# Input and up projections with the activations stationary: 512 weight columns stream, and TensorE turns the result back

## The reference

```
h = rms_norm(x, norm1_w);  proj = h @ w_in            # 2048 -> 5648: q, k, v, z, xbc (conv), dt
   attention (8 heads), SSD scan (16 heads)
x = x + concat(attn, ssm) @ w_out                     # 2048 -> 2048
h = rms_norm(x, norm2_w)
u = causal_dwconv(h @ w_up, ffn_conv_w, ffn_conv_b)   # 2048 -> 2 x 5632, 3 taps over positions
x = x + (silu(u_gate) * u_val) @ w_down               # 5632 -> 2048
second layer: mod = silu(c) @ w_ada + b_ada           # 2048 -> 6144, one row
h = rms_norm(x) * (1 + scale) + shift;  proj = h @ w_in_2   # 2048 -> 7168
   dilated attention (8 heads), retention (4 heads), gates
x = rms_norm(x + gate * (y @ w_out_2))
```

## Time and profile before

| | |
|---|---|
| median of 2 runs | 1643.15 us (1641.5 to 1644.81) |
| the profiled execution | 1646.69 us |
| its span, first to last instruction | 1645.0 us |
| TensorE matmul, VectorE, ScalarE busy | 1597.3, 1159.6, 807.7 us |
| mean granted clock of TensorE | 0.992 |
| HBM read | 332.8 MB, 204 GB/s over the span |

### The profile page before, as it was taken

One profiled execution on the slowest core, in us unless ns is written; L12 is line 12 of the kernel. 1 busy time (PEld: TensorE's weight loads), 2 busy tenths in 40 slices (PEclk: granted clock), 3 DMA queues, 4 the chain that ended last, 5 costly groups with the idle time before them and its releaser, 6 DMA issues.

```text
span 1645.0 us, 33704 instructions
## 1 busy us (share of the span) xinstructions
PE 1597.3 (97%) x13254; PEld 1567.6 (95%) x13254; DVE 1159.6 (70%) x1357; ACT 807.7 (49%) x973; POOL 26.3 (2%) x53
## 2 busy tenths in 40 slices
PE   7999999999999999999999999999799999999997
PEld 7998899989999999999999999999799999999996
DVE  6676677765678988888888888667664544664755
ACT  6444355544554545545545455444454544454542
POOL 0000000000000000000000000000000000000000
PEclk9999999999999999999999999999899999999999
DMA  9353344455548777787777875555455555455451
GB/s 347 137 180 129 128 153 142 154 184 185 184 160 335 271 271 297 258 303 274 258 290 270 302 288 188 189 187 183 141 188 185 189 184 168 139 170 174 156 180 52
DMA packets 85187, 336.17 MB, mean 204 GB/s; under 512 B 9456, under 2 KB 9712, under 8 KB 78704
## 3 DMA queue, kind: packets, MB, share of 16 engines
q1 hardware_dynamic: 77328, 281.05, 49.5%
q0 software_dynamic: 7056, 51.38, 8.5%
q10 hardware_dynamic: 720, 2.52, 0.4%
HBM read 332.82 MB, written 2.10 MB: 204 GB/s over the span
## 4 chain that ended last, share of the span: by engine, by line
PE 72%; DVE 5%; issue 2%; ACT 1%; DVEq 0%; ACTq 0%
PE PS L1097 23%; PE PS L1101 23%; PE PS L1099 23%; DVE ada_w L932 1%; DVE wlo L587 1%; ACT whi L255 1%; PE PS L1198 1%; DVE UV L890 1%; PE PS L1165 1%; PE PS L1343 0%; DVE X L1084 0%; PE PS L1184 0%; DVE rb L621 0%; DVE X L603 0%; PE PS L1144 0%
## 5 line engine op out<-in xcount | busy, mean ns | idle before, releaser
L1097 PE MATMUL PS<-gh,whi 128*128 128x256 f32 x3520 | 998.9, 284 | 14.6 <-DVE wlo L587 9.6
L1099 PE MATMUL PS<-gl,whi 128*128 128x256 f32 x3520 | 984.5, 280 | 0.0
L1101 PE MATMUL PS<-gh,wlo 128*128 128x256 f32 x3520 | 984.3, 280 | 0.0
L587 DVE TENSOR_TENSOR wlo<-raw,whi 128x1024 fp32r<-128x1024 f32 x528 | 644.7, 1224 | 421.1 <-ACT whi L255 420.0
L255 ACT ACTIVATE whi<-raw 128x1024 fp32r<-128x1024 f32 x528 | 557.7, 1060 | 718.5 <-PE PS L1101 716.1
L1097 PEld LDWEIGHTS PS<-gh,whi 128*128 128x128 f32 x3520 | 665.8, 189 | 21.9 <-issue 20.6
L1099 PEld LDWEIGHTS PS<-gl,whi 128*128 128x128 f32 x3520 | 667.2, 190 | 2.8 <-issue 1.9
L1101 PEld LDWEIGHTS PS<-gh,wlo 128*128 128x128 f32 x3520 | 667.4, 190 | 0.0
L1097 PE MATMUL PS<-ah,whi 128*128 128x256 f32 x704 | 198.8, 282 | 10.8 <-DVE UV L890 7.2
L1099 PE MATMUL PS<-al,whi 128*128 128x256 f32 x704 | 197.3, 280 | 0.0
L1101 PE MATMUL PS<-ah,wlo 128*128 128x256 f32 x704 | 197.3, 280 | 0.0
(11 more groups left out here) (187 smaller groups left out, 793.9 us busy)
## 6 DMA issues: line engine op xcount, KB each, us to landing
raw<-weights SPq DMA_DIRECT2D x528, 512.0 KB, 3.4
ada_w<-w_ada POOLq DMA_DIRECT2D x48, 1024.0 KB, 5.2
outT<-X SPq DMA_DIRECT2D x4, 512.0 KB, 2.6
X<-xT SPq DMA_DIRECT2D x3, 512.0 KB, 8.7
c<-const ACTq DMA_DIRECT2D x1, 1536.0 KB, 6.3
c_act<-c_rows POOLq DMA_DIRECT2D x1, 1024.0 KB, 9.0
X<-xT SPq DMA_DIRECT2D x2, 256.0 KB, 5.0
prm<-params ACTq DMA_DIRECT2D x1, 276.5 KB, 4.3
```

The source lines that it names most:

```text
L587: dve.tensor_tensor(wlo[:, j % SPLIT, :], raw[:, j, :], whi[:, j % SPLIT, :].bitcast(F32), ALU.subtract).then_inc(s_lo, 1)
L1097: pe.matmul(out[:, t, :], whi[:, b, w], hi[:, kt, :], start=first and half == 0 and t % 2 == 0, stop=False, skip_group_check=True)
L1099: pe.matmul(out[:, t, :], whi[:, b, w], lo[:, kt, :], start=False, stop=False, skip_group_check=True)
L1101: mm = pe.matmul(out[:, t, :], wlo[:, b, w], hi[:, kt, :], start=False, stop=last and half == 1, skip_group_check=True)
```

## The change

The input projections of both layers and the up projection use `product_natural`: now a tile of the activations (128 channels by 128 positions) is stationary and 512 weight columns stream, for each of 2 row tiles and 2 halves of the positions three matmuls, 12 per unit. A group then lies natural in its two banks: positions on the partitions, 512 channels along the free axis. It is turned back in these steps:

- ScalarE copies the two banks to SBUF (`natural`, in the up projection `ffn_natural` in two halves with the inverse root as its scale per partition), before the split of that slot.
- TensorE does the first unit of the next group and then eight transposes of 128x128 (`turn`). In the projections they write back into the group's own two banks, in the up projection into banks 4 and 5 (gate) and 6 and 7 (value). The value's turn stands behind the first unit of the down projection.
- `land` (VectorE, layer 1) and `landed2` (ScalarE, layer 2) take the turned group out, one slot later than before. In the up projection nothing is copied again: base and taps read PSUM, and the taps leave out the columns ahead of the first position, so that UG and UV with their zero columns go.

The inverse root of the second norm is needed per partition: `sum_columns` multiplies each half of the squares (stationary) with one column of ones, after the sixth unit of the first gate group. The convolution steps of layer 1 (`ssm_base`, `ssm_silu`, `ssm_taps`) come one slot later. The ada tiles are spread anew: 8 ahead of the loop (3 in the slots of the output projection, 5 in the first feed-forward step), then 4 in each of the 10 loop steps.

```diff
-        UG, o = place("UG", [P, 4, S + 2], offset=area)
-        UV, o = place("UV", [P, 4, S + 2], offset=o)
-        CG, o = place("CG", [P, 4, S], offset=o)
+        UN, o = place("UN", [P, 2, 4, S], offset=area)
+        CG, o = place("CG", [P, 4, S], offset=o + 64)
...
+            def natural(k, last, par, dst):
+                act.wait_ge(s_used, last + 1 + SPLIT)
+                act.activation(dst, acc_tiles(par), ACT.Copy).then_inc(s_nat, 1)
...
+            def ffn_natural(val, last, grp, par):
+                act.wait_ge(s_used, last + 1 + SPLIT)
+                act.wait_ge(s_evac, grp + 2)
+                for c in range(2):
+                    ins = act.activation(UN[:, val, 2 * c:2 * c + 2, :], acc_tiles(par)[:, 2 * c:2 * c + 2, :], ACT.Copy,
+                                         scale=r2[:, c:c + 1])
+                    ins.then_inc(s_unat, 1)
+                act.sem_inc(s_evac, 1)
...
             for n in range(IN_SLOTS):
+                if n % 8 == 7:
+                    natural(n // 8, 8 * B_IN + n, (G_IN + n // 8) % 2, landing1(n // 8))
                 split(B_IN, LEAD + n)
...
+            def landed2(g):
+                act.wait_ge(s_turn, 11 + g + 1)
+                act.activation(QB[:, 4 * g:4 * g + 4, :], acc_tiles((G_IN2 + g) % 2), ACT.Copy).then_inc(s_evac, 1)
...
             def land(g):
-                finished(8 * (B_IN + g) + 7, G_IN + g)
+                dve.wait_ge(s_turn, g + 1)
...
-                    if ada and j in (0, 3, 6):
-                        ada_tile(i, j // 3)
-                ffn_evac(unit + 7, grp, G_FF % 2, UG)
+                    if j in (3, 7):
+                        ada_tile(i, j // 4)
...
-                    if ada and j in (0, 6, 7):
-                        ada_tile(i, 3 + (0, 6, 7).index(j))
-                ffn_evac(unit + 15, grp + 1, (G_FF + 1) % 2, UV)
+                    if j in (0, 6):
+                        ada_tile(i, 2 + j // 6)
...
+            def product_natural(b, par, tiles, first, last):
+                for half in range(2):
+                    kt = tiles[half]
+                    w = slice(512 * half, 512 * half + 512)
+                    for c in range(2):
+                        rows = slice(P * c, P * c + P)
+                        out = PS[:, 2 * par + c, :]
+                        pe.matmul(out, gh[:, kt, rows], whi[:, b, w], start=first and half == 0, stop=False)
+                        pe.matmul(out, gh[:, kt, rows], wlo[:, b, w], start=False, stop=False)
+                        mm = pe.matmul(out, gl[:, kt, rows], whi[:, b, w], start=False, stop=last and half == 1)
+                mm.then_inc(s_used, 1)
+
+            def turn(src, dst, signal):
+                for c in range(2):
+                    for t in range(4):
+                        mm = pe.transpose(dst[:, t, P * c:P * c + P],
+                                          src[:, 2 * c + t // 2, P * (t % 2):P * (t % 2) + P], ident)
+                mm.then_inc(signal, 1)
...
+            def whole(blk, grp, par, need, after_first=None):
                 pe.wait_ge(s_evac, grp + 1)
+                for u in range(8):
+                    pe.wait_ge(s_lo, blk * 8 + (u + 1))
+                    pe.wait_ge(s_gl, need(2 * u + 1))
+                    product_natural(u % SPLIT, par, (2 * u, 2 * u + 1), u == 0, u == 7)
+                    if u == 0 and after_first is not None:
+                        ffn_turn(after_first, 0)
...
+            def sum_columns(buf):
...
+                    for c in range(2):
+                        mm = pe.matmul(PS[:, 4 + c, 0:1], buf[:, t // 4, t % 4, P * c:P * c + P], ones[:, 0:1],
+                                       start=(t == 0), stop=(t == 7))
...
             for n in range(IN_SLOTS):
                 stream_in(B_IN, G_IN, n, lambda kt: kt + 1)
+                if n % 8 == 0 and n:
+                    turned_back(n // 8 - 1, (G_IN + n // 8 - 1) % 2, landing1(n // 8 - 1))
                 slot1(n)
```

More of the change, by code:

```diff
@@ L965, in ffn @@
                         ffn_product(i)
-            dve.wait_ge(s_c, 1)
-            with dve.Fori(1, 1 + ADA_TILES // ADA_STEP) as i:
-                ffn(i, True)
-            for i in range(1 + ADA_TILES // ADA_STEP, FF_GROUPS):
+            with dve.Fori(1, last) as i:
                 ffn(i)
+            ffn(last)
             dve.wait_ge(s_ada, ADA_TILES)
@@ L1103, in product @@
                 mm.then_inc(s_used, 1)
-            def group(unit, j0, units, grp, par, hi, lo, need):
-                pe.wait_ge(s_evac, grp + 1)
-                for u in range(units):
-                    pe.wait_ge(s_lo, unit + (u + 1))
-                    if need is not None:
-                        pe.wait_ge(s_gl, need(2 * u + 1))
-                    product((j0 + u) % SPLIT, acc_tiles(par), (2 * u, 2 * u + 1), u == 0, u == units - 1, hi, lo)
-            def whole(blk, grp, par, need):
-                group(blk * 8, 0, 8, grp, par, gh, gl, need)
+            def product_natural(b, par, tiles, first, last):
[9 more added lines that the diff above has]
+                mm.then_inc(s_used, 1)
```

203 lines of the change are left out of this document (130 added, 73 removed).

## The result

The changed kernel takes 1673.7 us (median of 2 runs, 1673.12 to 1674.27) against 1643.15: a ratio of 1.022, 95% interval 1.018 to 1.027. It is 30.5 us slower where 40.5 us less were forecast. The miss is 71 us. Two runs each are few, for the kernel before ranges from 1631 to 1648 us over all its later runs. But both runs of the changed kernel are above 1673 us: it is slower, and only whether by more or less than 2% is unclear.

What follows compares the result with a forecast made beforehand. The prediction took TensorE's 128-column weight load to bound each pair, hiding the stream. Terms of -73.6 + 41.4 - 8.5 + 0.2 = -40.5 us gave a forecast of 1603 us from 1643.15, range 1592 to 1630 us.

Steps and rivals of the forecast that it cites:

- Natural products: Input and up projections: 4512 matmuls of 512 columns at 215.5 ns replace 9024 of 256, saving 73.6 us.
- The nearest rows: Earlier trace's F32 sum-of-squares instructions, 215 ns each, and 256-column matmuls at 1.2 GHz, 213 ns, taken to price wide products.
- rival 2: Wide products cost by the streamed column, 226.7 to 235.6 ns each: 1653 to 1693 us; loses from 224.5 ns; chance 0.08.
- Rival 1: Each change of weights costs wide products extra, 219.9 or 224.4 ns each: 1623 or 1643 us; chance 0.13.
- Turning back: Eight transposes for each of 47 groups on TensorE, 110 ns each: 41.4 us added.
- The copy: ScalarE's accumulator copy before each turn, 1.01 us, covered by the next group's first unit of 2.59 us: no cost.
- rivals 3 and 4: Late copies at 15 of 25 projection turns, +15 to +45 us (0.07); transposes at 274 ns latency, +62 us (0.02).
- Feed-forward on VectorE: Down projection's eight waits for UV and their restarts go, saving 8.5 us; 3.6 us at the last hi/lo split stays.
- One value wherever they stand: Sign to look for: 512-column F32R matmuls start 215 to 216 ns apart, the same in every stretch.
- What remains: The 152 units still using `product` keep about 421 us, -8 to +8 us, counted at nothing.
- Taps, base, alignment: Taps and base cost the same from PSUM as from SBUF, and activations keep their address offset: nothing added.

Runs made afterwards that it cites:

- e8: Changed kernel with 128 (first input projection) or 192 (up projection) streamed columns under 128-column loads, and 2 x 256 under 64-column loads (second input projection): 1521.1 us.
- e1: Changed kernel with streamed weights 320 columns wide in the first input projection, 384 in the up projection, 2 x 256 in the second input projection: 1528.0 us.
- e12: Changed kernel, middle units: up projection operands read as two-byte bfloat16, second input projection streaming one F32R column 512 times: 1653.5 us.
- e2: Changed kernel with weights stationary and 512 activation columns streaming in the second input projection, and alternating banks in the up projection: 1681.2 us.
- e3: Changed kernel with smaller stationary loads, 64 columns in the second input projection and 32 in the up projection: 1678.0 us.
- e7: Kernel before with only the new spread of the ada tiles: 1644.5 us, ratio 1.003 to the kernel before.
- e11: Kernel before run once more, unchanged: 1643.7 us.
- e13: Kernel before with the new ada spread and a redundant 512-column F32 matmul at three places: 1616.5 us, ratio 0.987 to the kernel before.
- e16: Kernel before with the new ada spread and a redundant 512-column F32R matmul ahead of each feed-forward step: 1619.7 us.
- e17: Changed kernel with a redundant 512-column F32 matmul at the second group of every down projection in the loop: 1675.1 us, ratio 1.022 to the kernel before.

## Why the prediction was wrong

- *Natural products, the step that failed.* The step had 215.5 ns; 230.3 were measured: +66.8 us. The change of stationary and moving was to save 73.6 us and saved 7. The step rested on the reading of the earlier trace rows, that a load of 113 ns bounds today's pair and hides its stream. e8 refutes it. A load of 128 columns and a stream of 256 are nearly equally long, so a row at 113 ns could not tell them apart, and I took the one that was written beside it.
- *The nearest rows.* The earlier trace rows read at half the rate, and I had said so myself, for rival 2. They have the same cycles but not the same bytes per time. The bound that speaks at full rate stood in the earlier trace rows: 0.443 ns a column.
- *Rival 2* gave 226.7 to 235.6 ns and 1653 to 1693 us, and is what happened (228.9 and 233.3 ns, 1674 us), at a chance of 0.08 where it deserved the most. Its mechanism was half right: the cost goes with the columns (e1, e8) and, as far as e12 tells, comes from reading new columns of SBUF, not from the streamed buffers being written (e2). Its other points held: the change loses from 224.5 ns on.
- *Rival 1*, a cost of each change of weights: out by the 216.3 ns of e12, with the same loads, and by e3, where a load of 32 columns leaves 231.6 ns. Against it speaks also the 427 ns at 1.2 GHz.
- *Turning back*, 41.4 us: 110 ns each measured, as forecast. *The copy* was late once, 1.4 us, so rivals 3 and 4 are out.
- *Feed-forward on VectorE*: the waits for UV went and 3.6 us stayed, as forecast, but in e7 the kernel gained nothing. A wait that also restarts the stream is not worth its length.
- *One value wherever they stand*, the prediction's sign for the wide products, was wrong too: they have two, as the narrower ones.
- *What remains*: 116.6 ns, +2.6 us of the 8 allowed for. *Taps, base, alignment*: nothing seen of a cost, as forecast.

## What to carry to other kernels

Before counting on a wider stream, find out which of load and stream bounds the pair, with a row in which only one of them is different; two durations that are nearly equal prove nothing. A duration from another format or another clock holds cycles, not bytes per time: price a stream by rows of its own format at its own rate. And when a long stretch of equal matmuls sits at one of two distances, try one odd matmul ahead of it before restructuring anything: it was worth 1.3% here, and the restructuring cost 2%.

## What was not expected of the hardware

- F32R streams a column in 0.443 to 0.460 ns at 2.4 GHz instead of 0.417 (229 to 233 ns for 512 columns), 216.3 ns if the column is repeated, 225.6 ns for two bytes a column.
- The same stream has two distances, 4.4 ns apart at 256 and at 512 columns alike. Once at one of them it stays there until it is interrupted, in e7 for 700 us; a distance of 142 ns among those of 118 changed it in two steps of e11, one of 144 ns at the same place in the kernel before didn't. Behind one added matmul of another width it was the lower one in each of the 33 places where e13 to e16 tried it, and in the ten of e17; one of the 33 was at it without (e7). Behind the sums of squares in the first up group (F32 of the products' own width) and behind the value's turn (eight transposes), 256 columns were at the higher one.
- Two operands' addresses against each other count for up to 5 ns a product; 64 bytes are best at 256 columns, 0 at 512.

Open: what the two distances are physically, why in the changed kernel 256 columns follow a turn at the higher and 512 columns at the lower one (in e2, with activations streaming, 512 columns follow it at the higher), whether a pause alone would set the value as an added matmul does, whether equal values from new addresses would stream as fast as a repeated column, and whether narrower values side by side (bfloat16 without the stride) would read at the full rate; no kernel here tried that.
